# Two transformer blocks on one core: a third weight slot, five row buffers, a recurrence in one block and attention in pairs

## The reference

```python
# first block, layer 0: gMLP mixer, then a mixture of experts on 768 tokens
# first block, layer 1: RWKV mixer (768 tokens in, 512 out), then experts on 512 tokens
def hier_moe(h, w_grp, b_grp, w_exp, b_exp, w_gate, w_up, w_down):
    ...   # a group of 4, then top 2 of its 8 experts, for each token
    return (jax.nn.silu(xb @ w_gate[e]) * (xb @ w_up[e])) @ w_down[e]   # 32 experts, 1024 -> 512 -> 1024

def _wkv_step(S, inp):            # for 16 heads of 64 and both directions
    r_t, w_t, k_t, v_t, a_t, b_t = inp
    sa = jnp.einsum('zbhvk,zbhk->zbhv', S, a_t)
    S = S * w_t[..., None, :] + sa[..., :, None] * b_t[..., None, :] + v_t[..., :, None] * k_t[..., None, :]
    return S, jnp.einsum('zbhvk,zbhk->zbhv', S, r_t)

# second block, layer 0: 8 heads of a window of 128 with sinks beside 8 dilated heads (64 units of attention)
# second block, layer 1: latent attention, 16 heads, causal over 512 tokens (64 units)
```

## Time and profile before

| | us |
|---|---|
| median of 3 runs (4344.81 to 4356.38) | 4351.2 |
| the profiled run, and its span | 4352.07, 4350.3 |
| the span to the end of the gMLP mixer | 0 to 671 |
| norm, routing, experts, combine, layer 0 | 674 to 1474 |
| RWKV norm and projections | 1476 to 1823 |
| recurrence | 1824 to 2716 |
| RWKV output | 2726 to 2833 |
| norm, routing, experts, combine, layer 1 | 2834 to 3552 |
| second block: window attention within | 3797 to 3890 |
| second block: latent attention within | 4157 to 4268 |

### The profile page before, as it was taken

One profiled execution on the slowest core, in us unless ns is written; L12 is line 12 of the kernel. 1 busy time (PEld: TensorE's weight loads), 2 busy tenths in 40 slices (PEclk: granted clock), 3 DMA queues, 4 the chain that ended last, 5 costly groups with the idle time before them and its releaser, 6 DMA issues. The chain is left out here.

```text
span 4350.3 us, 104061 instructions
## 1 busy us (share of the span) xinstructions
PE 3608.8 (83%) x46088; PEld 2318.8 (53%) x46088; DVE 1254.8 (29%) x2935; ACT 779.1 (18%) x1781; POOL 619.4 (14%) x794
## 2 busy tenths in 40 slices
PE   4999994999995189878888887769999919987787
PEld 2445543655553045467777777345656504464464
DVE  2131114111110530055555554531111130161253
ACT  1011001000000100143333332010000010151152
POOL 0000000111110100054444442001111110000000
PEclk7999995999998599889999999879999959998988
DMA  7741104999998422200000000369999933201010
GB/s 272 286 165 39 73 20 177 354 386 391 386 384 300 121 86 77 71 15 16 18 20 18 18 18 12 113 245 394 395 387 389 375 139 96 87 9 65 24 40 25
DMA packets 303038, 707.10 MB, mean 163 GB/s; under 512 B 26829, under 2 KB 50349, under 8 KB 301964
## 3 DMA queue, kind: packets, MB, share of 16 engines
q1 hardware_dynamic: 268036, 613.55, 38.3%
q0 software_dynamic: 25840, 71.67, 5.0%
q10 hardware_dynamic: 8728, 15.34, 0.9%
HBM read 648.20 MB, written 52.31 MB: 161 GB/s over the span
## 5 line engine op out<-in xcount | busy, mean ns | idle before, releaser
L901 PE MATMUL banks<-w_gate_up_ring,x_turned 128*32 128x256 f32 x12288 | 694.7, 382 | 37.1 <-DMA w_gate_up_ring<-in_moe_w_up_dram 35.6
L901 PEld LDWEIGHTS banks<-w_gate_up_ring,x_turned 128*32 128x32 f32 x12288 | 431.2, 110 | 273.8 <-issue 61.2
L919 PE MATMUL banks<-w_down_ring,hidden_turned 128*32 128x256 f32 x6144 | 344.8, 380 | 0.0
L977 DVE TENSOR_TENSOR hidden<-silu_gate,banks 128x128 f32<-128x128 f32 x192 | 55.2, 287 | 773.8 <-ACT silu_gate L957 737.8
L878 POOL DMA_DIRECT2D y_rows<-y_out_rows x256 | 141.5, 560 | 950.4 <-ACT y_out_rows L963 915.4
L919 PEld LDWEIGHTS banks<-w_down_ring,hidden_turned 128*32 128x32 f32 x6144 | 193.7, 110 | 128.1 <-issue 0.2
L337 PE MATMUL banks<-const_cols,h_tokens 128*128 128x128 f32 x240 | 54.4, 407 | 247.9 <-DVE h_tokens L310 162.2
L1914 DVE TENSOR_TENSOR inverse_both_ways<-banks,inverse_both_ways 128x512 f32<-128x512 f32 (+1 forms) x240 | 152.1, 637 | 253.1 <-PE banks L1823 252.2
L866 POOL DMA_INDIRECT x_rows<-h_rows,cell_index x64 | 62.7, 980 | 914.0 <-POOLq L42 887.7
L456 PE MATMUL banks<-gmlp_weights,h_turned_gmlp 128*128 128x512 f32 x384 | 174.9, 611 | 12.0 <-DMA gmlp_weights<-in_ga_w_in_dram 12.0
L337 PEld LDWEIGHTS banks<-const_cols,h_tokens 128*128 128x128 f32 x240 | 45.7, 217 | 257.3 <-DVE h_tokens L310 169.8
(11 more groups left out here) (457 smaller groups left out, 5336.9 us busy)
## 6 DMA issues: line engine op xcount, KB each, us to landing
w_gate_up_ring<-in_moe_w_gate_dram SPq DMA_DIRECT2D x70, 2048.0 KB, 8.8
w_gate_up_ring<-in_moe_w_up_dram SPq DMA_DIRECT2D x70, 2048.0 KB, 24.0
w_down_ring<-in_moe_w_down_dram SPq DMA_DIRECT2D x70, 2048.0 KB, 16.6
u_channels<-in_ada_w_dram SPq DMA_DIRECT2D x40, 1024.0 KB, 6.9
y_rows<-y_out_rows POOLq DMA_DIRECT2D x256, 96.0 KB
gmlp_weights<-in_ga_w_in_dram SPq DMA_DIRECT2D x8, 2048.0 KB, 8.3
ab_weights<-in_ab_w_in_dram SPq DMA_DIRECT2D x6, 2048.0 KB, 8.5
ada_first<-in_ada_w_dram SPq DMA_DIRECT2D x2, 4096.0 KB, 17.6
```

Of the source, the lines that this page charges most:

```text
L901: last = pe.matmul(ps[strip(j), GU + g, 0:2 * FQ].rearrange("p (a c) -> p a c", a=2), xT[:, e % 2, k, strip(g)], wgu[:, e % 2, :, k, j * F ...
L919: last = pe.matmul(ps[strip(j), Y + g // 2, (g % 2) * DQ:(g % 2 + 1) * DQ], hT[:, g, strip(k)], wd[:, e % 2, k, j * DQ:(j + 1) * DQ], star ...
```

## The change

1. **norm_turn** with stores has five row buffers and five `kept` semaphores. SyncE waits for all stores at the end of its list in this block; the waits in `route` go.
2. **experts**: three separate slots for gate and up, the third allocated when the turned rows are freed and loaded by SyncE in the block of `route`. SyncE's order is now down(2), gate/up(3), down(3), gate/up(4), ...; gate/up of e waits for the sums of e - 3 and stands behind down of e - 1, which waits for the products of e - 3. One semaphore per slot. The stores of y move from POOL's to ScalarE's list, behind waits for `y_low` and `y_high`. The blocks beyond use slot 2 (`SPARE`).
3. **recurrence**: one block for everything. Semaphores count on through the pairs (`Counted`), without clearing. All 24 rounds stand in one loop. SyncE issues the loads for c + 1 early. The lora products, the norm's and the bonus's share one bank, each waiting until the one before is moved. Scan reads share a bank. In a round: P1 is gone as one product; XM gives L, copied by ScalarE (four copies of half the partitions, rows crossed over) and written into X by `copy_predicated` on VectorE, whose buffers XI hold the identity from the start; POOL makes all LQn at the start of the round from the copied L and does no X work, but adds the identity to F, which ScalarE moves out. Rows are placed so that the two products of XX use two quadrants each that are different ones. MV and WU loop over the four combinations. RB, TA, TB, TK and MV stand inside levels 1 to 4. One of the two copies of WU moves to VectorE. A step of the preparation is taken by ScalarE in these levels behind its copies.
4. **attention**: four score banks (0 to 3), two for transposes, two for outputs; four score and four probability buffers. TensorE takes two units at a time: two scores, two transposed, two products with values. In the window layer the units of a pair of heads alternate.

```diff
@@ norm_turn
-        h = sb("h_tokens", [P, 2, D])
-        junk = sb("squares", [P, D])
+        deep = 2 if keep is None else KEPT
+        h = sb("h_tokens", [P, deep, D])
+        junk = sb("squares", [P, D]) if keep is None else h[:, deep - 1, :]
...
+                if keep is not None:
+                    for r in range(min(n, deep)):
+                        sp.wait_ge(kept[r], 16 * len(range(r, n, deep)))
...
@@ moe and route
-        wgu = sb("w_gate_up_ring", [P, 2, 2, KD, F])
+        wgu = [sb(f"w_gate_up{r}", [P, 2, KD, F]) for r in range(2)]
...
+        wgu.append(sb("w_gate_up2", [P, 2, KD, F]))
...
-                sp.wait_ge(kept[0], 16 * ((nt + 1) // 2))
-                sp.wait_ge(kept[1], 16 * (nt // 2))
+                load_third(sp)
...
@@ experts
                 for e in range(2, E):
                     r = e % 2
-                    sp.wait_ge(gu_sum, GROUPS * (e - 1))
-                    sp.dma_start(wgu[:, r, 0, :, :], gate_src[e]).then_inc(gate_in[r], 16)
-                    sp.dma_start(wgu[:, r, 1, :, :], up_src[e]).then_inc(up_in[r], 16)
+                    if e > 2:
+                        sp.wait_ge(gu_sum, GROUPS * (e - 2))
+                        sp.dma_start(wgu[e % 3][:, 0, :, :], gate_src[e]).then_inc(gu_in[e % 3], 16)
+                        sp.dma_start(wgu[e % 3][:, 1, :, :], up_src[e]).then_inc(gu_in[e % 3], 16)
                     sp.wait_ge(y_sum, 2 * (e - 1))
                     sp.dma_start(wd[:, r, :, :], down_src[e]).then_inc(down_in[r], 16)
...
-                    pool.wait_ge(y_low, e + 1)
-                    pool.wait_ge(y_high, e + 1)
-                    for j in range(QUARTERS):
-                        pool.dma_start(y_blocks[e, j], ys[strip(j), r, :, :]).then_inc(y_out[r], 16)
...
+                    act.wait_ge(y_low, e + 1)
+                    act.wait_ge(y_high, e + 1)
+                    for j in range(QUARTERS):
+                        act.dma_start(y_blocks[e, j], ys[strip(j), e % 2, :, :]).then_inc(y_stored[e % 2], 16)
...
@@ Prepare on TensorE
+                    done = 4 * n + 2 * z + half
+                    if done:
+                        self.wait(pe, "sig_done", done)
+                    pe.matmul(ps[:, 7, 0:H2], w[part, :], src[part, half * H2:(half + 1) * H2], start=True, stop=True).then_inc(s["lora_sum"], 1)
...
@@ the rounds
+        beside = {1: ["RB"], 2: ["TA"], 3: ["TB", "TK"], 4: ["MV"], 5: []}
...
+        to_row = lambda h, cc: row[cc ^ h]
+        from_row = lambda h, cc: row[cc ^ h ^ 1]
...
+                                for cc in range(2):
+                                    last = pe.matmul(ps[from_row(h, cc), 4 * h + 1, u * CHUNK:(u + 1) * CHUNK], LQ[h][to_row(h, cc), n - 1, u, :],
+                                                     X[h][to_row(h, cc), 0, u, :], start=True, stop=True)
+                            PE.mark(last, products, f"Z{n}_{h}")
...
+                                    here = from_row(h, cc)
+                                    if n < last_lv:
+                                        pe.matmul(ps[to_row(h, cc), 4 * h, u * CHUNK:(u + 1) * CHUNK], X[h][here, 1, u, :], Z[h][here, u, :], start=True, stop=True)
+                                    last = pe.matmul(ps[here, 4 * h + 1, (4 + u) * CHUNK:(5 + u) * CHUNK], Z[h][here, u, :], X[h][here, 1, u, :], start=True, stop=True)
...
+                        DVE.mark(dve.copy_predicated(by_dir(XI[h][:, 0, :, :]), both("x0", 2, CHUNK).bitcast(U32), by_dir(fours(ps[:, 4 * h + 1, low]))),
...
+                    for n in lv:
                         for h in range(2):
+                            pool.wait_ge(by_act, ACTS.of(f"L_{h}", R))
+                            POOL.mark(pool.tensor_tensor(by_dir(LQ[h][:, n - 1, :, :]), by_dir(L[h][:, :, :]), quarters(n), ALU.mult), by_pool, f"LQ{n}_{h}")
...
@@ attention
+                for i in range(0, n + 4, 2):
+                    for m in (i, i + 1):
+                        if m < n:
+                            q, k = units[m][0], units[m][1]
+                            pe.matmul(ps[:, m % SUMS, 0:width(m)], q, k, start=True, stop=True).then_inc(scores_sum, 1)
+                    for j in (i - 2, i - 1):
...
+                    for j in (i - 4, i - 3):
...
```

More of the change, by code:

```diff
@@ L640 @@
 ROUTER = NG + E
+KEPT = 5
+SPARE = E % 3
 LOGITS = 4
@@ L1796, in _ @@
-                    for h in range(2):
-                        wait(by_dve, DVE, f"MR_{h}")
-                        for u, (z, ti) in enumerate(units):
-                            for cc in range(2):
-                                last = pe.matmul(ps[row[cc], 4 * h + 2, u * CHUNK:(u + 1) * CHUNK], MR[h][row[cc], u, 0, :],
-                                                 b["V"][row[cc], pair[ti], h * 64:(h + 1) * 64], start=True, stop=True)
-                        PE.mark(last, products, f"MV_{h}")
@@ new lines, in _ @@
+                        if n == 4:
+                            if rnd == 0:
+                                prepare[c].wait(pe, "v_in", 16)
+                            wait(by_act, ACTS, "TK")
+                            for u, (z, ti) in enumerate(units):
+                                for h, cc in quads:
+                                    last = pe.matmul(ps[from_row(h, cc), 4 * h + 2, u * CHUNK:(u + 1) * CHUNK], MR[h][row[cc], u, 0, :],
+                                                     b["V"][row[cc], pair[ti], h * 64:(h + 1) * 64], start=True, stop=True)
+                            PE.mark(last, products, "MV")
@@ L1853, in _ @@
+                    PE.mark(last, products, "WU")
+                    if rnd == 0:
+                        next(ahead, None)
+                    wait(by_act, ACTS, "WU_0")
+                    wait(by_dve, DVE, "WU_1")
                     if lat:
@@ L1929, in _ @@
                     next(ahead, None)
-                    dve.wait_ge(products, PE.of("F", rnd))
-                    for cc in range(2):
-                        at = slice(2 * pair[0] + cc, 2 * pair[1] + cc + 1, 2)
-                        last = dve.tensor_tensor(out["F"][:, :, at, :], by_dir(fours(ps[:, 4 * cc + 2, 0:4 * CHUNK])),
-                                                 c_("ident64").unsqueeze(1).unsqueeze(1).to_broadcast([P, DIRS, 2, CHUNK]), ALU.add)
-                    DVE.mark(last, by_dve, "F")
-                    next(ahead, None)
-                run(ahead)
-                run(behind)
+                    if rnd == 2:
+                        late = ahead
+                run(scan[KD - 1].on_vector(dve))
             @block.scalar
@@ L1977, in _ @@
                         ACTS.skip(act, by_act, "YC")
-                    if rnd == 0:
+                    need("F")
+                    for cc in range(2):
+                        at = slice(2 * pair[0] + cc, 2 * pair[1] + cc + 1, 2)
+                        last = copy(out["F"][:, :, at, :], by_dir(fours(ps[:, 4 * cc + 2, low])))
+                    ACTS.mark(last, by_act, "F")
+                    if rnd < 2:
                         next(ahead, None)
-                run(ahead)
+                scan[KD - 1].on_scalar(act)
```

1101 lines of the change are left out of this document (562 added, 539 removed).

## The result

The changed kernel takes 4294.7 us (median of 4 runs, 4284.4 to 4298.4) against 4348.0 for the kernel before beside it: a ratio of 0.9869, interval 0.9850 to 0.9888. So 53 us went where 174 were forecast, and the time lies 40 us over the range's upper end of 4255. The profiled run took 4298.39, its span is 4296.4.

A forecast was written before the change was run, and what follows sets the result against it. TensorE was taken to bound the recurrence, with a copy chain close behind, and DMA the experts. Savings of 148.7 (recurrence), 16.9 (norm and experts) and 8 (attention), 173.6 off 4352.1, gave 4178 us; range 4105 to 4255.

The forecast's parts named there:

- Part 3, a round: Recurrence: a round takes 23.2 us against 29.1, with four-quadrant products shortening TensorE's work and a 2.56 us chain setting levels.
- Part 3, a middle pair: Recurrence: three rounds of 69.6 us plus preparation of the next pair make 87.0 us, against 105.3 before.
- The bounds: Recurrence: a middle pair lies between 79 and 96.6 us, so the whole part saves 197 to 91.
- Part 1, norm: Norm of layer 0: five row buffers end VectorE's wait, SyncE closes the block at 714.4, 6.2 us saved.
- Third slot: Experts: earlier weight loads give a net lead of 4.2 us a layer, counted in full, plus 1 a layer.
- Stores of y: Experts: moving these stores to ScalarE's list costs 0, bounds -0.3 and +0.13 us an expert.
- Part 4, attention: Both attentions: units in pairs remove about half of TensorE's waits for VectorE's outputs, 8 us; bounds 3 and 16.
- Rivals. 1: Recurrence: ScalarE's preparation steps find room between its copies, 52 us less, total 4126; chance 0.2.
- Rival 3: Recurrence: XX, MV and WU don't run four abreast, each round keeps 5.3 us, total 4305; chance 0.06.
- rival 2: Recurrence: the chain from bank to bank limits nearly everywhere, a middle pair takes 96.6 us, total 4241; chance 0.2.
- Rival 4: Recurrence: short waits in every level lose TensorE's high clock, slower than before, 4352 and more; chance 0.04.
- A: Theory from the experiments' expectations: instruction supply limits TensorE where it runs four abreast; savings in passes only become pauses.

The follow-up runs named there:

- e4: Kernel before plus independent 64x64 products behind layer 1's experts: two quadrants 91.1 us, four 85.4 us for the same work.
- e6: Changed kernel with the stores of y issued by GpSimd (POOL) again: 4306.8 us, ratio 0.9887 to 0.9918.
- e11: The changed kernel run once more, unaltered: 4289.9 us, ratio 0.9834 to 0.9882.
- e3: Kernel before with only the new attention and its order of units: 4334.2 us against 4351.6, ratio 0.9954.
- e5: Changed kernel with idle 128-column products added in each pair's first round only: 4301.7 us, ratio 0.9863 to 0.9899.
- e10: Changed kernel with every product of a recurrence round made in two quadrants at a time: 4308.0 us, ratio 0.9894 to 0.9931.

## Why the prediction was wrong, step by step
- **What bounds the kernel.** Right in the place (recurrence, TensorE first, a chain behind it), incomplete in the list of limits. The row that would have told stands in the page of before as well: the instruction queue, 364 packets of 16 KB. And the earlier trace rows show L1780 four abreast for one group of 30 passes only, which one block holds. The step that failed is the term of TensorE's passes in a round: it took the pace of a burst (15 ns a pass) for a pace that lasts, where 256 instructions, 128 passes, come no faster than each 3.56 us (e4). And its sum put the cost of the lower clock at nothing.
- **Part 3, a round.** Forecast 23.2, the round shown took 30.8: to the first XX 5.85 (3.7), levels 18.0 (14.2), the rest 6.9 (5.3). Its four pauses make 5.4; 25.4 are left.
- **Part 3, a middle pair.** Forecast 87.0, six are 522. Semaphore waits and passes at full clock measured 158.6 + 359 = 518 (502 by the second count), so the sum of what it counted was right to some per cent. That is partly luck, as two slips cancel: rounds are some 2 us longer than forecast and the preparation adds 11 instead of 17 a pair. What it did not count, pauses of 62 and a clock of 43, 105 us together, is the whole of the miss of 100. In the first pair (83.0 against 100.9) they are 8.7 and 10.7, in the last (69.6 against 87.1) the pauses are 12.0.
- **The bounds.** 79 and 96.6 both varied how the parts of the chain overlap. None came from a resource that the new pace would reach, so the measured 103.75 lay outside, and so does the 101.8 of e6, the shortest profile of the same pairs.
- **Part 1, norm.** Forecast end 714.4, set by SyncE. Columns as in the earlier trace rows:
```profile
702.99 8.59 SPq L686 DMA_DIRECT2D w_down_ring<-in_moe_w_down_dram  x1
...
703.38 3.47 PE L330 MATMUL banks<-router_w,h_turned 128*128 128x36 f32 x16
708.40 6.88 PE L330 MATMUL banks<-router_w,h_turned 128*128 128x36 f32 x32
```
SyncE ends at 711.58, the logits at 715.28, at a granted clock of 0.50 from 690 us on. The wait is gone as said; the clock closes the block in this profile. From the norm's start to the end of the logits it is 43.2 us, 46.9 before: 3.7 saved, forecast 6.2. Of the eleven profiles with five buffers, six have the logits at full clock; they end at 703 to 705 there, and SyncE's issue closes the block (at 712.5 in e11), as forecast.
- **Part 2, experts.** The sum was near, two terms of it wrong. Third slot: forecast 10.4 in all. e6 has it without the moved stores: its blocks take 593.2 and 593.5 us, the one before 596.0 and 593.0, and e3 and e4, with the same two slots, 591.5 to 592.3. So no gain shows. The step that failed is "it counts in full, since DMA sets the end": in the changed kernel TensorE is busy 563 of the 580 us of layer 0, and the idle time that it spends on weights there was 19.8 us before and is 12.2, so little was left to gain. Stores of y: forecast 0; e6 against the changed kernel says 10.2 (5.7 + 4.5), 7.8 of it behind the last copy. The move was priced by ScalarE's idle time and the DMA share in the middle of the loop; what counted was the last store of all, which nothing covers. The Trainium skill (Trainium Kernel Development and Optimization, Key Constraints) says that issuing from several engines saves only issue time. Inside the loop the trace agrees, with a DMA share of 1.04 and 580.3 us to the last copy of y against 582.4 in e6; at the end of the block the measurement differs from it, by 4 us a block.
- **Part 4, attention.** Forecast 8, bounds 3 and 16, measured 17. In the latent part the wait went nearly wholly (6.3 to 0.2 us), not by half, and the idle time that is left elsewhere shrank too: 103.0 to 92.5 at the same clock of 0.97. The profile before had 111.9 at a clock of 0.88; those 9 us are not the order's, and the rows of one profile did not tell them apart.
- **Rivals.** 1 and 2 are not met as put. Rival 3's time (4305) is the nearest, but its mechanism is false: XX starts 32 passes in 0.47. Behind rival 2 stood the Trainium skill (TensorEngine Tiling (Array Packing), Performance Considerations, PSUM Bottleneck), by which the copies out of PSUM may become the limit. Such copies do end waits here (of w_and_u 10.7 us, of Z's step 10.7 in the six pairs), but the idle time with a named releaser fell from 77 to 67 us, so no run here shows that limit reached. Rival 4 had the right cost, the clock, in the wrong place and size: the low level grew from 37.5 to 126 us in six pairs, worth 29, and lies mostly in the first round of each pair, not in every level.

What stays open: what exactly lowers the clock. In every middle pair of the profile the longest stretch at the lower level begins 4 to 9 us after the first product of the pair's first round (at 2066.3 after 2057.8, at 2165.3 after 2161.4), not 14 to 19 as e5's text has it, behind waits for POOL, the lora products and their copies; TensorE is busy 0.64 of the time in those first microseconds. Fills there halve it. The pauses of e4 did not lower it, and e10, with few pauses, still has 68 us. Nor was a version tried that needs fewer instructions, which would be the direct test of A in this kernel.

## What to carry to other kernels
Before you price a faster order of small products, count instructions, weight loads and both fp32 passes too, and ask how fast they can be brought: here no faster than 256 in 3.5 us for long. A burst in the trace shorter than one such block proves nothing on the lasting pace. Price the last transfer of a block apart from the same transfer in its loop. And profile the same stage more than once before a few microseconds are put down to a change: here four profiles of the same six pairs lie 13 us apart, by the clock alone.

## What was not expected of the hardware
- Instructions reach TensorE in blocks of 16,384 bytes (256); over 24 blocks in a row one came each 3.56 us, 27.8 ns for a pass with its weight load, whatever the quadrants could do (15 ns in a burst). In the recurrence the 38 longer pauses of six pairs all stand at the same place of a block.
- The same work, packed tighter, was granted less clock: 68 us at the low level with two quadrants, 92 with XX in four, 99 to 140 in four profiles with all. What in it lowers the clock is not shown.
- At a block's end stores issued by ScalarE let the next block start 5.7 to 7.7 us after the end of the last copy, those by GpSimd 10.0 to 10.8.
